# Two transformer blocks on one core: VectorE takes over weight remainders and square sums

## The reference, cut to what matters

```
swiglu(x, w_gate, w_up, w_down) = (silu(x @ w_gate) * (x @ w_up)) @ w_down      # 1024 -> 2816 -> 1024

for l in range(2):
    x = x + 0.5 * swiglu(rms_norm_2(x, ffn1_norm[l]), ffn1_w_gate[l], ffn1_w_up[l], ffn1_w_down[l])
    h = rms_norm_2(x, mix_norm[l])
    z = h @ w_in[l]                       # queries, keys, values of two attentions; gates zg
    o_na, o_sw = two attentions of z
    g = sigmoid(zg + b_gate[l])
    merged = g[0] * (o_na @ w_branch_na[l]) + g[1] * (o_sw @ w_branch_sw[l])
    x = x + merged @ w_out[l]
    x = x + 0.5 * swiglu(rms_norm_2(x, ffn2_norm[l]), ffn2_w_gate[l], ffn2_w_up[l], ffn2_w_down[l])
```

## Time and profile before

| | |
|---|---|
| median of 3 runs | 3227.32 us (3227.09 to 3229.16) |
| the profiled execution: time, span | 3222.49 us, 3220.7 us |
| busy share: TensorE, VectorE, ScalarE, GpSimd | 90%, 60%, 46%, 28% |
| mean granted TensorE clock | 0.944 of full speed |
| GpSimd's 128x1024 remainders, line 550 | 180, mean 2489 ns |
| VectorE's 128x1024 remainders, line 2341 | 132, mean 1288 ns |

### The profile page before, as it was taken

How to read it: one execution, slowest core, us unless ns; L and a number is a source line. 1 busy time by engine, 2 the same in 40 slices (tenths; PEclk the granted TensorE clock), 3 DMA queues, 4 the chain that set the end, 5 groups by cost and what they waited for, 6 DMA issues and landing times. The chain is left out here.

```text
span 3220.7 us, 47223 instructions
## 1 busy us (share of the span) xinstructions
PE 2890.6 (90%) x16210; PEld 2455.1 (76%) x16210; DVE 1948.3 (60%) x2496; ACT 1479.3 (46%) x2185; POOL 911.9 (28%) x467
## 2 busy tenths in 40 slices
PE   4888869997699997998989999999988979989999
PEld 3755657776599875776879997899866767779987
DVE  7544268786788434752268865788354662288843
ACT  3251337775555333653345543555334653355532
POOL 2430201111132352212443325232442113443233
PEclk8997969998899998998999999999999989999999
DMA  7710249997133223111322223132231102222222
GB/s 277 267 39 1 92 163 351 340 356 288 53 105 104 85 85 111 46 33 53 106 77 98 99 100 110 65 105 91 92 137 49 44 26 78 98 81 102 99 85 98
DMA packets 95234, 377.43 MB, mean 117 GB/s; under 512 B 10832, under 2 KB 11104, under 8 KB 92896
## 3 DMA queue, kind: packets, MB, share of 16 engines
q1 hardware_dynamic: 89072, 348.69, 31.1%
q0 software_dynamic: 4608, 16.78, 1.3%
q10 hardware_dynamic: 1456, 10.66, 0.8%
HBM read 363.50 MB, written 16.78 MB: 118 GB/s over the span
## 5 line engine op out<-in xcount | busy, mean ns | idle before, releaser
L550 POOL TENSOR_TENSOR w_lo<-raw,w_hi 128x1024 fp32r<-128x1024 f32 x180 | 447.8, 2489 | 1117.0 <-ACT w_hi L670 1117.0
L1651 PE MATMUL pb<-bl,g_wh 128*128 128x256 f32 x2464 | 711.2, 289 | 39.7 <-DVE bl L2390 16.5
L1652 PE MATMUL pb<-bh,g_wl 128*128 128x256 f32 x2464 | 702.9, 285 | 0.0
L1653 PE MATMUL pb<-bh,g_wh 128*128 128x256 f32 x2464 | 702.4, 285 | 0.0
L1651 PEld LDWEIGHTS pb<-bl,g_wh 128*128 128x128 f32 x2464 | 478.4, 194 | 50.2 <-issue 33.4
L1652 PEld LDWEIGHTS pb<-bh,g_wl 128*128 128x128 f32 x2464 | 478.9, 194 | 1.8 <-issue 1.7
L1653 PEld LDWEIGHTS pb<-bh,g_wh 128*128 128x128 f32 x2464 | 478.5, 194 | 0.0
L1322 PE MATMUL pb<-hl,w_hi 128*128 128x512 f32 (+1 forms) x688 | 284.6, 414 | 55.7 <-DVE hl L1950 21.8
L670 ACT ACTIVATE w_hi<-raw 128x1024 fp32r<-128x1024 f32 x196 | 206.4, 1053 | 238.5 <-PE pb L1324 210.4
L1323 PE MATMUL pb<-hh,w_lo 128*128 128x512 f32 (+1 forms) x688 | 273.6, 398 | 0.0
L1324 PE MATMUL pb<-hh,w_hi 128*128 128x512 f32 (+1 forms) x688 | 273.4, 397 | 0.0
(11 more groups left out here) (417 smaller groups left out, 5929.1 us busy)
## 6 DMA issues: line engine op xcount, KB each, us to landing
raw<-in_wstream SPq DMA_DIRECT2D x220, 512.0 KB, 3.5
m_raw<-in_moe_stream SPq DMA_DIRECT2D x192, 512.0 KB, 6.5
g_own<-in_gu_stream SPq DMA_DIRECT2D x44, 768.0 KB, 4.3
raw<-in_gu_stream SPq DMA_DIRECT2D x44, 768.0 KB, 4.2
ada_ring<-in_ada SPq DMA_DIRECT2D x8, 2048.0 KB, 8.0
g_own<-in_gu_stream SPq DMA_DIRECT2D x44, 256.0 KB, 3.0
hidf<-in_gu_stream SPq DMA_DIRECT2D x44, 256.0 KB, 3.1
adaw<-in_ada SPq DMA_DIRECT2D x4, 2048.0 KB, 23.0
```

The lines of the kernel that those rows point to most:

```text
L550: pool.tensor_tensor(w_lo[s][:], raw[s][:], w_hi[s][:].bitcast(F32), ALU.subtract).then_inc(w_lod, 1)
L1651: pe.matmul(o, lh, rl, start=first and k == 0, stop=False, skip_group_check=True)
L1652: pe.matmul(o, ll, rh, start=False, stop=False, skip_group_check=True)
L1653: m = pe.matmul(o, lh, rh, start=False, stop=k == 3, skip_group_check=True)
```

## The change

VectorE makes the remainders of the weights of the four down products, of the merge from its third chunk on and of the output product, and it adds the squares. GpSimd keeps the sums S1 and S3 and the remainders of the projections and heads. VectorE's queue gets the new operations at these places: `low(b0, 0)` in the last pair behind `up_hi`, `low(b0, 1)` behind that pair, later ones behind `f_low` of the same chunk; in the merge two ahead of the products and one ahead of the merged tile's own remainder; in the output product behind the add to x. The first two hidden halves are scaled and split before the last gate/up pair, into a tile `f01` of their own (it lies where `g_own` was). ScalarE doesn't wait for that pair's second product any more. In feed-forward 2, `first_pair` is ahead of the output product on ScalarE and VectorE instead of behind its first two chunks. GpSimd's sums for the next feed-forward come as soon as the load has landed.

```
@@ f_hi_of
-            if type(k) is not int or k < LATE:
+            if type(k) is not int or 2 <= k < LATE:
                 return fh[:, s, :]
+            if k < 2:
+                return f01[:, k, :]
@@ GpSimd, per feed-forward
-                    with pool.Fori(0, 4) as j:
-                        low_pair(b0 + j)
-                    if f == 1:
+                    if h == 0:
+                        pool.wait_ge(w_lod, 2 * (b0 + NF // 2))
+                        with pool.Fori(NF // 2, O_MG // 2 + 1) as j:
+                            low_pair(b0 + j)
+                    if Q0 + NF < NQ:
                         add_gu(Q0 + NF, n0 + NF // 2, 0)
...
@@ (low_pair, low_tail, low_one and add_squares are gone from this queue)
@@ ScalarE, end of gate/up
                 pair(Q0 + NF - 2, NF - 2, n0 + NF // 2 - 1, (NF - 2) % 6)
+                for s in range(2):
+                    f_split(s, s)
                 pair(Q0 + NF - 1, NF - 1, n0 + NF // 2 - 1, (NF - 1) % 6, last=True)
-                act.wait_ge(g_used, 7 * (Q0 + NF - 1) + 9)
                 for s in range(2):
                     hi(b0, s)
-                    f_split(s, s)
@@ ScalarE, output product
+                first_pair(Q0, n0)
                 for s in range(2):
                     hi(wo + 1, s)
                     take(f, s)
                 split_early(f, 0)
-                first_pair(Q0, n0)
@@ VectorE, new helpers (low_tail and add_squares move here unchanged but for the engine)
+            def low(pair, s):
+                dve.wait_ge(w_hid, 2 * pair + s + 1)
+                dve.tensor_tensor(w_lo[s][:], raw[s][:], w_hi[s][:].bitcast(F32), ALU.subtract).then_inc(w_lod, 1)
@@ VectorE, pair
+                    if last:
+                        f_low(0, 0)
+                        f_low(1, 1)
+                        dve.wait_ge(w_lod, 2 * b0)
                     up_hi(Q, c)
                     if not last:
                         lo_s31(Q + 1, 1 - u)
+                    else:
+                        low(b0, 0)
                     gate_hi(Q, k, c)
                     scale(Q, k)
@@ VectorE, end of gate/up and down
-                pair(Q0 + NF - 1, NF - 1, n0 + NF // 2 - 1, (NF - 1) % 6, last=True)
                 for s in range(2):
                     f_scale(s)
-                    f_low(s, s)
+                pair(Q0 + NF - 1, NF - 1, n0 + NF // 2 - 1, (NF - 1) % 6, last=True)
+                low(b0, 1)
                 hidden(Q0 + NF - 1, NF - 1, NF - 1)
                 with dve.Fori(0, LATE // 2 - 1) as j:
                     for s in range(2):
                         f_scale(2 * j + 2 + s)
                         f_low(2 * j + 2 + s, s)
+                        low(b0 + 1 + j, s)
                 for k in range(LATE, NF):
                     f_scale(k)
                     f_low(k, k % 2)
+                    low_tail(b0, k)
@@ VectorE, adds to x behind a down product (and with m in (2, 4, 5) at the start of layer 1)
                     x_add(2 * l, m)
+                    if m >= 2:
+                        add_squares(3 * l + 1, m - 1)
@@ VectorE, merge
+                        for n in range(2):
+                            cn = 3 * mm + n
+                            low(mb + 3 * i + (cn + 2) // 2, cn % 2)
                         dve.wait_ge(mg_gate, 2 * (M + 1))
...
                         dve.tensor_tensor(mg_tile(mm), gate_tile(mm, 0), gate_tile(mm, 1), ALU.add).then_inc(mg_f, 1)
+                        low(mb + 3 * i + (3 * mm + 4) // 2, mm)
                         dve.wait_ge(mg_hi, M + 1)
@@ VectorE, output product
+                def w_out(c):
+                    dve.wait_ge(w_used, 2 * wb + c + 1)
+                    dve.tensor_tensor(x[:, c, :], pb[1 + c % 2][:], x[:, c, :], ALU.add).then_inc(x_ready, 1)
+                    if c >= 2:
+                        add_squares(norm_of(f), c - 1)
+                    if c + 2 < KD:
+                        low(wb + c // 2 + 1, c % 2)
-                w_out_pair(0)
+                first_pair(Q0, n0)
+                w_out(0)
+                w_out(1)
                 low_early(f, 0)
-                first_pair(Q0, n0)
                 ... (w_out(2) to w_out(7) in the places of w_out_pair(1) to (3))
```

More of the change, by code:

```diff
@@ L599, in _ @@
             add_gu(0, 0, 0)
[L601 to L617, removed]
             for l in range(NL):
@@ L627, in _ @@
                             add_gu(Q0 + 2 * i + u, n0 + i, u)
-                    with pool.Fori(0, 4) as j:
-                        low_pair(b0 + j)
-                    if f == 1:
-                        add_gu(Q0 + NF, n0 + NF // 2, 0)
[L632 to L650, removed]
+                    if h == 0:
[3 more added lines that the diff above has]
+                    if Q0 + NF < NQ:
+                        add_gu(Q0 + NF, n0 + NF // 2, 0)
         @block.scalar
@@ L1729, in down @@
                                 pe.wait_ge(g_hid, Q0 + NF + 3)
[L1730 removed]
+                            ins = mm3(pb[m][:], w_hi[s][:, m, :], w_lo[s][:, m, :], f_hi_of(k, s), row(fl, k),
                                       first and s == 0, False)
@@ L2424, in rs_of_norm, with low_tail, add_squares @@
                 dve.wait_ge(rs_ready, 3 + n + 1)
+            def low(pair, s):
+                dve.wait_ge(w_hid, 2 * pair + s + 1)
+                dve.tensor_tensor(w_lo[s][:], raw[s][:], w_hi[s][:].bitcast(F32), ALU.subtract).then_inc(w_lod, 1)
+            def low_tail(b0, k):
+                to_hi, to_lo = w_of(k)
+                dve.wait_ge(w_hid, 2 * b0 + k + 1)
+                dve.tensor_tensor(to_lo, raw[k % 2][:], to_hi.bitcast(F32), ALU.subtract).then_inc(w_lod, 1)
+            def add_squares(n, j):
+                dve.wait_ge(sq_ready, 3 * KD + KD * n + j + 1)
+                if j > 1:
+                    dve.wait_ge(sq_sum, ADDS[n] + j - 1)
+                dve.tensor_tensor(rs[:], stemp[:] if j == 1 else rs[:], root_ring[j % 2], ALU.add).then_inc(sq_sum, 1)
             def ffn(f, Q0, n0, b0):
@@ L2646, in _ @@
                 mb = lb + O_MG // 2
+                dve.wait_ge(w_lod, 2 * mb + 2)
                 with dve.Fori(0, KD // 2) as i:
@@ L2662, in _ @@
                 wb = lb + O_WO // 2
-                def w_out_pair(i):
-                    for s in range(2):
-                        dve.wait_ge(w_used, 2 * (wb + i) + s + 1)
-                        dve.tensor_tensor(row(x, 2 * i + s), pb[1 + s][:], row(x, 2 * i + s), ALU.add).then_inc(x_ready, 1)
                 f, Q0, n0 = 2 * l + 1, 2 * NF * l + NF, NF * l + NF // 2
-                w_out_pair(0)
+                def w_out(c):
[8 more added lines that the diff above has]
+                w_out(1)
                 low_early(f, 0)
-                first_pair(Q0, n0)
-                w_out_pair(1)
+                w_out(2)
+                w_out(3)
                 low_early(f, 1)
-                w_out_pair(2)
+                w_out(4)
+                w_out(5)
                 low_late(f, 2)
-                w_out_pair(3)
+                w_out(6)
+                w_out(7)
                 ffn(f, Q0, n0, lb + O_F2 // 2)
@@ L2683, in _ @@
                         x_add(f, m)
+                        if l + 1 < NL and m in (2, 4, 5):
+                            add_squares(norm_of(f + 1), (1, 2, 3)[max(0, m - 3)])
                     if l + 1 < NL and g < 2:
```

3 lines of the change are left out of this document (2 added, 1 removed).

## The result

The changed kernel takes 3190.91 us, the median of 4 runs (3187.05 to 3193.70), against 3227.63 us (3227.09 to 3229.16) before on the same chip: a ratio of 0.9885, 95% interval 0.9868 to 0.9902. The forecast was 3195.0, range 3182 to 3209. The profiled execution of after has a span of 3191.9 us (before: 3220.7).

A forecast was written before the change was run, and what follows sets the result against it. TensorE, busy 90% of the span, was taken as the bound, leaving only its waits at stage borders and its half clock. The terms summed to 32.3 us off the median 3227.3, giving 3195.0, range 3182 to 3209.

The forecast's parts named there:

- 1: Start of the down product, four times: gap freed, new stall of 1.25 us; gains 4.8 us, plus 1.7 of clock once.
- 2: Tail of the down product, four times: faster remainders gain 6.4 us, plus 3.4 for half of the lost clock.
- 3: Norm behind the down product, twice: the last square sum queues behind VectorE's last x add; loses 0.8 us each, 1.6 in all.
- 7: Second layer's start, once: the gap of 5.16 us becomes 3.6; gains 1.6 us, plus 0.4 for the clock.
- 4: Merge to output product, twice: the merge's sum falls from 2.76 to 0.69 us; gains 4.0 us, plus 0.8 of clock.
- 5: Output product, twice: moving first_pair earlier removes a 3.4 us wait and the half clock behind it; gains 10.2 us.
- 6: Output product to gate/up, twice: last remainder comes earlier but two GpSimd sums still collide; gains 0.3 us each, 0.6 in all.
- (a): Rival: the port comes free, GpSimd's sums miss VectorE's operations and the tails keep the clock; about 3183 us, chance 0.12.
- (b): Rival: early scales and splits in the last gate/up pair cost what they save, clock falls; about 3205 or 3208 us, chance 0.17.
- (c): Rival: VectorE becomes the bound in down, merge and output product; overrun by 0.3 us a remainder gives 3239 us, chance 0.04.
- (d): Rival: nothing moves, removed gaps come back as later ones because only hidden work changed hands; 3227 us, chance 0.04.

The follow-up runs named there:

- the second execution: The changed kernel run once more without any edit, beside the combined versions on the same chip: 3189.42 us, ratio 0.989 to the kernel before.

## Why the prediction was right, point by point

The sum was 32.3 us; the profiled executions are 28.8 apart, the medians 36.7. The total came right with two terms too small (1 and above all 2, 5.4 us together) and two too large (3 and 7, about 8 us). That they nearly cancelled was luck.

**1. Start of the down product: right.** Forecast 4.8 + 1.7. The gap fell by 2.4 each, the new stall is 1.04 instead of 1.25, released by ScalarE's line for part 0 as walked: 4 x (2.4 - 1.04) = 5.4. The third down product, which alone had half clock behind its start, is 5.00 us shorter instead of 3.5 to 4.0, so its 1.7 are there too.

**2. Tail: the mechanism was right, the size too small.** Forecast 2.45 each with half of the clock. The one wait is 1.49 instead of 2.0, and all four tails keep the clock where two were counted, which is 3.4 of the 4.8 us. The down products are 3.84, 3.53, 3.30 (5.00 less the 1.7) and 3.96 shorter: 14.6 instead of 9.8. The cycle of 3.5 us was right (3.47 measured).

**3. Norm: the step that failed.** Forecast a loss of 0.8 each, as if the sum took its 0.69 us. It took 2.81, because GpSimd's first remainder of the projections starts at the same moment: ScalarE makes that high part as soon as TensorE's last chunk lets it. In before, GpSimd's own square sum kept the two apart. TensorE's product of the last square starts 5.8 and 5.1 us behind the start of the last down matmul, 1.8 before: 3.9 and 3.3 us lost, 7.2 in all, and a little more with the half clock in which these products ran. With GpSimd held back the loss was 0.9 each, so the step was right for the sum's place in the queue and put the collision at nothing. The prediction named this contention as a price and didn't apply it here; the lower bound of the term, -2.6, was missed by far.

**4 and 5. Merge and output product: right.** The wait fell from 5.99 to 4.06 (forecast 4.0), the merge's sum to 0.69, the wait in the output product is gone with its half clock. Forecast 15.0 for both terms, measured 3.9 for the wait and 4.7 + 6.2 inside the output product: 14.8. One reason was wrong in part: the wait in the output product was called `first_pair`'s doing, and 3.4 us were to come back if it ran late. Its early place is enough to remove the wait with either engine's remainders, but the late order with VectorE's remainders brings back only 1.77 of 3.4 us.

**6. Output product to gate/up: right.** 3.06 became 2.60 (forecast 0.3 each).

**7. Second layer's start: failed.** Forecast 5.16 to 3.6, measured 5.23 (4.97 in the second execution). VectorE's queue sets this border, not TensorE: between 1997 and 2027 VectorE is busy 27.8 of 30 us (window, VectorE busy, granted clock, DMA share, GB/s):

```profile
1997.00:2011.00 14.00, 13.12 (x15) 1.00 0.47 151
2011.00:2027.00 16.00, 14.64 (x25) 0.86 0.00 0
```

So a TensorE that gets there sooner only waits longer. The down product ahead of it came out 3.5 us shorter where the sum had 2.45. The version with GpSimd's remainders in the down products points the same way: a down product 3.2 us longer, and a wait 1.4 us shorter. Where VectorE's own queue gets shorter (the next scale ahead of the remainder), the wait fell together with the down product, to 4.02. So at most 1.1 of the missing 1.6 us (an estimate: 3.5 less 2.45) is the tail's gain, given back at a border that another engine sets; the rest wasn't settled, and 0.3 of it lies between two executions of one kernel. Holding the sums took 2.8 us off this wait, so the contention at this border was real; how much of it the forecast of 3.6 had counted isn't on record.

**The rivals.** (a) came true in one part: the tails kept the clock. That the sums miss VectorE's operations did not happen by itself; holding them gave 3185.9. (b) is out: no clock was lost at the new stalls. (c) is out: the down product goes at 0.2256 us a matmul up to the tail. (d) holds for term 7 alone.

## What to carry to other kernels

When a remainder or a sum moves from GpSimd to VectorE, list what GpSimd will start instead in the next microsecond: the engine that was freed ran its next operation into VectorE's last one and cost 2.1 us at the norm, twice. An operation that only fills a wait belongs ahead of the one that waits (the sum of square 6 ahead of the last add, the next scale ahead of the remainder, the scales behind the pair's own parts): three such changes of order and one hold gave 25 us, two thirds of what the whole change gave. A time that moves by 3 us is looked up in its stage before it is believed, since the clock alone moves one border by that much.

## What the hardware showed that was not expected

- The same wait doesn't bring the same clock. Behind waits of 2.6 and 2.5 us at one border the granted clock was 0.51 and 0.50 in one execution of the kernel and 1.00 in another (2.58 and 2.31 us). The one wait of 1.49 us in a tail left the clock at 1.00 in the two windows shown, and in none of the four tails was there half clock; two waits of 1.2 and 1.8 with 1.0 us of work between them were followed by 0.54 and 0.55.
- Beside GpSimd's operations, VectorE's with two SBUF inputs grew from 0.69 us to 1.67, 1.77 and 2.81, and GpSimd's sums of 128x512 from 1.29 to 1.6 to 1.7; VectorE's adds to x, which read PSUM, stayed at 0.68 at the same place.
